# A decoder block in fp32 parts on one Trainium2 core: later first weight load, another count of unread transposes, one unit in another order, one product on another engine

## The chip, the cores and the metric

The kernel is one program on one core of a Trainium2 chip. The metric is the device time of one execution in microseconds (us). A core has five engines that run their own instruction streams beside each other and wait for each other by semaphores: TensorE (PE in the rows, its weight loads PEld), VectorE (DVE), ScalarE (ACT), GpSimd (POOL) and SyncE (SP), which here only issues DMA transfers.

## The reference

One layer of a hybrid block on x of 512 tokens by 1024 channels, all in float32. Cut to what matters:

```python
h = rms_norm(x, pre_mix_g)
q, k, v, u_pool, u_conv, g_logits = split(h @ w_in)
attn = moba_attention(q, k, v, rel_bias) @ w_attn_o
pool = pool_mixer(u_pool, w_pool_g, pool_scale) @ w_pool_o
conv = conv_module(u_conv, w_dw, b_dw, ln_g, ln_b) @ w_conv_o
gates = sigmoid(g_logits + b_gate)
x = x + rms_norm((gates[0]*attn + gates[1]*pool + gates[2]*conv) @ w_out, post_mix_g)
h = rms_norm(x, pre_ffn_g)
gt, up = split(h @ w_ffn_in)
f = (silu(gt) * up) @ w_ffn_out
out = x + rms_norm(f, post_ffn_g)
```

The two places of the change are the very first line with the first products behind it (the two halves of u_conv), and the last line.

## The kernel before

Every product is made of three matmuls on parts: a value is split into a high part (rounded by ScalarE on the way through a copy) and a low part (what is left, a subtraction on VectorE), and hi by hi, hi by lo and lo by hi are added up in one PSUM bank. A unit is one weight tile of 1024 by 128: it is loaded into one of the three slots of `raw` by SP (line 323), ScalarE writes `w_hi` (598) and VectorE `w_lo` (1004), and TensorE runs 8 steps k of three matmuls of 512 columns (1556 to 1558).

**The start.** SP issues the four token tiles of 128 tokens (`x_tok`, 326), then the weight loads of units 0 to 2 with the vector table `vec` behind the first of them (336), then four small loads. For each token tile ScalarE squares and sums (617), GpSimd takes the power -0.5 (451), VectorE scales the tile (1027) and TensorE turns it in eight transposes (1572), one into each PSUM bank. Between them stand unread transposes of the identity into bank 5 (1577): 20 in front of tile 0, 5 in front of tiles 2 and 3, none in front of tile 1. Behind the last tile's eighth transpose the same transpose is repeated 14 times. Then, bank by bank, ScalarE writes `h_hi` (629) and VectorE `h_lo` (1037), and unit 0 begins as soon as the first of these is there. Of the low parts of units 0 and 1 VectorE writes the first half and GpSimd the second (455). TensorE starts a unit when `lo_done` says that the low part is there; within units 0 and 1 it waits for GpSimd's half at step 4.

**The end.** The last product (f by w_ffn_out) is built as seven half-size products in 39 units; the sums of the products are four quadrants of the output, c11, c12, c21 and c22 (tokens by channels, halves each), where c22 is finished during unit 35. ScalarE squares a quadrant's two tiles and sums them, the gain vector `post_ffn_g` is multiplied in, and at the very end VectorE multiplies by 1/rms and adds the residual (`add_x1`, 1509). GpSimd multiplies c11, c21 and c22 by the gain (572); c12, the last one, is multiplied on VectorE (1544). After the products GpSimd also takes the reciprocal roots (`final_rstd`, 575 to 579). VectorE's queue over the last units is a list written by hand: for each unit n the low part of its weights (`down_lo`, 1451), the low part of the token side (`s_lo`, 1461), and at fixed n the additions to the quadrants. TensorE takes units 36 to 38 first for token tile 0 and then again for token tile 1 (1896 to 1903).

The order on each engine is the order in which the code is written; no scheduler stands between.

Of the kernel before, what the change touches and what calls it, by code (L numbers as in the profile page):

```python
# [29 lines left out]
P = 128  # L30
SEQ = 512
# [104 lines left out]
def build(nc, x, w_in, w_branch, w_out, w_ffn_in, w_ffn_out, vecs, post_mix_g, pre_ffn_g, post_ffn_g,  # L136
# [98 lines left out]
    with ExitStack() as ctx:  # L235
        bank = [ctx.enter_context(nc.psum_tensor(f"bank{i}", [P, SEQ], F32)) for i in range(8)]

        def sem(name):
# [49 lines left out]
            sem("u4_full"), sem("y1_full"), sem("c_gained"), sem("y_gained"), sem("out_ready"))  # L288

# [28 lines left out]
        def _(sp):  # L318
# [8 lines left out]
            first = [COL_CONV + 256, COL_CONV, COL_CONV + 384, COL_CONV + 128, COL_POOL, COL_POOL + 128]  # L327
            for u, col in enumerate(first):
# [6 lines left out]
                if u == 0:  # L335
                    sp.dma_start(vec[:, :], vecs).then_inc(vec_full, 16)
# [99 lines left out]
        def _(pool):  # L436
# [132 lines left out]
            for i, (c, half) in enumerate(((c11, 0), (c21, 0), (c22, 1))):  # L569
                for t in range(2):  # L570
                    pool.wait_ge(sq_done, 16 + 2 * i + t + 1)
                    pool.tensor_tensor(c[:, t, :], c[:, t, :], gain[:, half * SEQ:(half + 1) * SEQ], ALU.mult)\  # L572
                        .then_inc(c_gained, 1)
# [426 lines left out]
        def _(dve):  # L1000
# [511 lines left out]
            for n in range(2, DOWN_UNITS):  # L1512
# [19 lines left out]
                if n == C22_MADE:  # L1532
                    dve.wait_ge(p_moved, 6)
                    add_product(c22, PH_P7)

            for t in range(2):
                dve.wait_ge(rstd_done, 12 + t + 1)
                dve.wait_ge(c_gained, 6)
                add_x1(c21, t, 2 + t, 0)
                add_x1(c22, t, 2 + t, 1)  # L1540
# [12 lines left out]
        def _(pe):  # L1553
# [20 lines left out]
            for t in range(TOK):  # L1574
                if t != 1:
                    for _ in range(5 if t else 20):
                        pe.transpose(bank[5][:, SEQ - P:SEQ], ident[:, :], ident[:, :])
                pe.wait_ge(xn_done, t + 1)
                for k in range(KT):
                    ins = turn_tile(t, k)  # L1580
                    if t == TOK - 1:
                        if k == KT - 1:
                            for _ in range(14):
                                ins = turn_tile(t, k)
                        ins.then_inc(xt_done, 1)
# [3 lines left out]
            def first_k(u):  # L1589

                def before(k):
                    if u == 0:
                        pe.wait_ge(h_lo_done, k + 1)
                    if k == KT // 2:
                        pe.wait_ge(low_rest_done, u + 1)
                return before

            for u in range(FIRST_UNITS):
                pe.wait_ge(lo_done, u + 1)
                if u >= RING:  # L1600
                    pe.wait_ge(*FIRST_FREED[u - RING])
                unit(u % RING, bank[u % RING], h_hi, h_lo, before_k=first_k(u) if u < 2 else None).then_inc(unit_done, 1)
# [368 lines left out]
```

## Time and profile before

| | us |
|---|---|
| median of 3 runs (708.35 to 708.84) | 708.79 |
| the profiled execution | 707.53 |
| its span, first to last instruction | 705.3 |
| TensorE busy | 695.8 |
| VectorE busy | 533.8 |
| ScalarE busy | 359.6 |
| GpSimd busy | 238.0 |

The profiled execution is 1.26 us shorter than the median; every number from the trace belongs to it. Starts are in us from the first instruction. A matmul row has a start and a modelled duration that overlaps the next one, so the distance from start to start is the pace, and a hole is a distance above it. A duration on VectorE or GpSimd includes what the instruction waits for after its start.

### The profile page before, as it was taken

How to read it: one execution, taken by the hardware profiler on the slowest of the kernel's cores; microseconds unless marked ns; L12 is line 12 of the kernel's file. 1: busy time of each engine (PE TensorE's matmuls, PEld its weight loads, DVE VectorE, ACT ScalarE, POOL GpSimd, SP SyncE). 2: the span in 40 equal slices, each digit the busy share in tenths (PEclk: the TensorE clock that was granted, in tenths of full speed). 3: DMA queues.
4: the chain of work that ended last, by engine and by line, in shares of the span. 5: the costliest groups of instructions: out<-in, count | busy, mean ns of one | idle time of the engine just before them, and what ended most of it. 6: DMA issues, size and time to landing. Idle time of an engine off the chain costs nothing.

```text
span 705.3 us, 11497 instructions
## 1 busy us (share of the span) xinstructions
PE 695.8 (99%) x4056; PEld 616.8 (87%) x4056; DVE 533.8 (76%) x776; ACT 359.6 (51%) x582; POOL 238.0 (34%) x213
## 2 busy tenths in 40 slices
PE   8999999999999999999999999999999999999996
PEld 7888888888888888888889999999999999888884
DVE  5338878578666666788478988887888787898997
ACT  7235544544544655234367454555455546655672
POOL 3842211112220000562222556665566550000125
PEclk9999999999999999999999999999999999999999
DMA  6158899999985213234403133313322334665563
GB/s 247 60 210 237 226 238 227 233 267 217 231 206 148 93 61 119 90 100 162 192 26 120 60 120 119 105 74 119 119 103 76 119 119 151 191 196 199 169 206 127
DMA packets 37678, 107.24 MB, mean 152 GB/s; under 512 B 4041, under 2 KB 4041, under 8 KB 37457
## 3 DMA queue, kind: packets, MB, share of 16 engines
q1 hardware_dynamic: 29648, 83.79, 34.4%
q0 software_dynamic: 8000, 23.07, 15.2%
q8 instruction: 17, 0.28, 0.2%
q14 instruction: 13, 0.10, 0.0%
HBM read 104.73 MB, written 25.19 MB: 184 GB/s over the span
## 4 chain that ended last, share of the span: by engine, by line
PE 96%; DVE 1%; DMA 1%; ACT 0%; issue 0%; POOL 0%; SPq 0%; DVEq 0%; POOLq 0%; ACTq 0%
PE bank L1556 30%; PE bank L1558 30%; PE bank L1557 30%; PE bank L1622 1%; DMA x_tok<-in_x_dram 1%; PE bank L1612 1%; PE bank L1613 1%; PE bank L1639 1%; PE bank L1638 1%; DVE w_lo L1451 1%; PE bank L1766 1%; PE bank L1572 0%; DVE s_lo L1461 0%; PE bank L1629 0%; DVE c L1500 0%
## 5 line engine op out<-in xcount | busy, mean ns | idle before, releaser
L1556 PE MATMUL bank<-h_hi,w_hi 128*128 128x512 f32 (+1 forms) x392 | 149.6, 382 | 0.0
L1558 PE MATMUL bank<-h_hi,w_lo 128*128 128x512 f32 (+1 forms) x392 | 147.6, 377 | 0.0
L1557 PE MATMUL bank<-h_lo,w_hi 128*128 128x512 f32 (+1 forms) x392 | 147.5, 376 | 0.0
L1004 DVE TENSOR_TENSOR w_lo<-raw,w_hi 128x1024 fp32r<-128x1024 f32 (+1 forms) x54 | 70.6, 1308 | 58.5 <-ACT w_hi L606 46.2
L1558 PEld LDWEIGHTS bank<-h_hi,w_lo 128*128 128x128 f32 x392 | 73.8, 188 | 13.7
L1556 PEld LDWEIGHTS bank<-h_hi,w_hi 128*128 128x128 f32 x392 | 73.8, 188 | 13.0 <-DVE w_lo L1004 0.4
L1557 PEld LDWEIGHTS bank<-h_lo,w_hi 128*128 128x128 f32 x392 | 73.9, 188 | 12.6
L1556 PE MATMUL bank<-tm_hi,blk_hi 128*128 128x256 f32 x240 | 67.9, 283 | 0.0
L1557 PE MATMUL bank<-tm_lo,blk_hi 128*128 128x256 f32 x240 | 67.9, 283 | 0.0
L1558 PE MATMUL bank<-tm_hi,blk_lo 128*128 128x256 f32 x240 | 67.9, 283 | 0.0
L1385 DVE TENSOR_TENSOR blk_lo<-raw_pair,blk_hi 128x512 fp32r<-128x512 f32 (+1 forms) x40 | 59.5, 1488 | 7.4 <-ACT blk_hi L863 7.4
L1556 PE MATMUL bank<-w_hi,s_hi 128*128 128x512 f32 x154 | 60.1, 390 | 0.9 <-DVE s_lo L1461 0.9
L863 ACT ACTIVATE blk_hi<-raw_pair 128x512 fp32r<-128x512 f32 (+1 forms) x40 | 33.7, 841 | 52.5 <-DVE raw_pair L1391 52.5
L555 POOL TENSOR_TENSOR w_sum<-raw_pair 128x512 f32<-128x512 f32 x20 | 32.2, 1612 | 83.4 <-DMA raw_pair<-in_w_ffn_in_dram 83.4
L1557 PE MATMUL bank<-w_lo,s_hi 128*128 128x512 f32 x154 | 59.9, 389 | 0.0
L1558 PE MATMUL bank<-w_hi,s_lo 128*128 128x512 f32 x154 | 59.9, 389 | 0.0
L888 ACT ACTIVATE w_hi<-raw 128x1024 fp32r<-128x1024 f32 (+1 forms) x39 | 40.9, 1049 | 33.1 <-PE bank L1558 33.1
L1451 DVE TENSOR_TENSOR w_lo<-raw,w_hi 128x1024 fp32r<-128x1024 f32 (+1 forms) x39 | 50.1, 1284 | 9.9 <-ACT w_hi L888 9.8
L606 ACT ACTIVATE w_hi<-raw 128x1024 fp32r<-128x1024 f32 x46 | 48.4, 1052 | 3.9 <-PE bank L1558 3.7
L572 POOL TENSOR_TENSOR c<-c,gain 128x512 f32<-128x512 f32 x6 | 11.5, 1931 | 103.3 <-ACT junk L617 103.3
L1556 PEld LDWEIGHTS bank<-tm_hi,blk_hi 128*128 128x128 f32 x240 | 46.1, 192 | 0.0
L1557 PEld LDWEIGHTS bank<-tm_lo,blk_hi 128*128 128x128 f32 x240 | 46.1, 192 | 0.0
(233 smaller groups left out, 1779.8 us busy)
## 6 DMA issues: line engine op xcount, KB each, us to landing
raw<-in_w_in_dram SPq DMA_DIRECT2D x42, 512.0 KB, 4.9
raw_pair<-in_w_ffn_in_dram SPq DMA_DIRECT2D x40, 512.0 KB, 3.7
comb<-in_w_ffn_out_dram POOLq DMA_DIRECT2D x30, 512.0 KB, 7.1
raw<-comb SPq DMA_DIRECT2D x20, 512.0 KB, 3.6
raw<-in_w_ffn_out_dram SPq DMA_DIRECT2D x15, 512.0 KB, 3.7
comb<-comb POOLq DMA_DIRECT2D x10, 512.0 KB, 5.1
raw<-in_w_branch_dram SPq DMA_DIRECT2D x8, 512.0 KB, 3.2
raw<-in_w_out_dram SPq DMA_DIRECT2D x8, 512.0 KB, 3.2
```

What stands on the lines that cost most here:

```text
L555: pool.tensor_tensor(w_sum[:, 0, :], m21, m22, ALU.add).then_inc(w_summed, 1)
L572: pool.tensor_tensor(c[:, t, :], c[:, t, :], gain[:, half * SEQ:(half + 1) * SEQ], ALU.mult)\
L606: act.activation(w_hi[:, hslot, :], raw[:, slot, :], ACT.Copy).then_inc(hi_done, 1)
L863: act.activation(dst, src, ACT.Copy).then_inc(blk_hi_done, 1)
L888: act.activation(w_hi[:, down_slot(n), used], raw[:, u % RING, used], ACT.Copy).then_inc(hi_done, 1)
L1004: dve.tensor_tensor(dst, src_hi[0], src_hi[1], ALU.subtract).then_inc(lo_done, 1)
L1385: dve.tensor_tensor(dst, src, part.bitcast(F32), ALU.subtract).then_inc(blk_lo_done, 1)
L1451: dve.tensor_tensor(w_lo[:, down_slot(n), used], raw[:, u % RING, used], w_hi[:, down_slot(n), used].bitcast(F32), ALU.subtract).then_inc( ...
L1556: pe.matmul(dst, a_hi, b_hi, start=start, stop=False, skip_group_check=resumed)
L1557: pe.matmul(dst, a_hi, b_lo, start=False, stop=False, skip_group_check=resumed)
L1558: return pe.matmul(dst, a_lo, b_hi, start=False, stop=stop, skip_group_check=resumed)
L1612: pe.matmul(bank[3 + i % 2][:, 0:w], q_parts[:, head, q], k_hi2[:, head, 0:w], start=True, stop=False)
```

## The change

Four edits. (1) SP: `vec` is loaded directly behind the token tiles, and the three weight loads wait until token tile 1 has landed (`x_full[1]`). (2) TensorE: the unread transposes are 27, 0, 3, 3 in place of 20, 0, 5, 5, and the last tile's repeats are 7 in place of 14. (3) TensorE: unit 1 runs its 16 matmuls with the high part of the weights first, waiting for that part alone, and then the 8 with the low part. (4) The product of c22 by the gain moves from GpSimd to VectorE, one token tile behind unit 36 and the other behind unit 37, under a new semaphore.

```diff
+            sp.dma_start(vec[:, :], vecs).then_inc(vec_full, 16)
+            sp.wait_ge(x_full[1], 16)
             for u, col in enumerate(first):
...
-                if u == 0:
-                    sp.dma_start(vec[:, :], vecs).then_inc(vec_full, 16)
...
-            for i, (c, half) in enumerate(((c11, 0), (c21, 0), (c22, 1))):
+            for i, c in enumerate((c11, c21)):
                 for t in range(2):
                     pool.wait_ge(sq_done, 16 + 2 * i + t + 1)
-                    pool.tensor_tensor(c[:, t, :], c[:, t, :], gain[:, half * SEQ:(half + 1) * SEQ], ALU.mult)\
+                    pool.tensor_tensor(c[:, t, :], c[:, t, :], gain[:, 0:SEQ], ALU.mult)\
                         .then_inc(c_gained, 1)
...
+                if n in (C22_MADE + 1, C22_MADE + 2):
+                    t = n - C22_MADE - 1
+                    dve.wait_ge(sq_done, 16 + 4 + t + 1)
+                    dve.wait_ge(gain_full, 48)
+                    dve.tensor_tensor(c22[:, t, :], c22[:, t, :], gain[:, SEQ:], ALU.mult).then_inc(c22_gained, 1)
...
-                dve.wait_ge(c_gained, 6)
+                dve.wait_ge(c_gained, 4)
                 add_x1(c21, t, 2 + t, 0)
+                dve.wait_ge(c22_gained, t + 1)
                 add_x1(c22, t, 2 + t, 1)
...
-                    for _ in range(5 if t else 20):
+                    for _ in range(3 if t else 27):
...
-                            for _ in range(14):
+                            for _ in range(7):
...
+            def high_parts_first(u):
+
+                pe.wait_ge(hi_done, u + 1)
+                for k in range(KT):
+                    w1 = w_hi[:, u % RING, k * P:(k + 1) * P]
+                    pe.matmul(bank[u % RING][:, :], w1, h_hi[:, k, :], start=k == 0, stop=False)
+                    pe.matmul(bank[u % RING][:, :], w1, h_lo[:, k, :], start=False, stop=False)
+                pe.wait_ge(lo_done, u + 1)
+                for k in range(KT):
                     if k == KT // 2:
                         pe.wait_ge(low_rest_done, u + 1)
-                return before
+                    ins = pe.matmul(bank[u % RING][:, :], w_lo[:, u % RING, k * P:(k + 1) * P], h_hi[:, k, :],
+                                    start=False, stop=k == KT - 1)
+                return ins
...
+                if u == 1:
+                    high_parts_first(u).then_inc(unit_done, 1)
+                    continue
```

SP's queue at the start, before; `x_tok` are the token tiles, `raw` the weight slots:

```order
L326 DMA x_tok<-in_x_dram 128x1024 x4
L323 DMA raw<-in_w_in_dram 128x1024
L336 DMA vec<-in_vecs_dram 128x102
L323 DMA raw<-in_w_in_dram 128x1024 x2
L338 DMA table<-in_rel_bias_dram 8x32
```

and after the change:

```order
L327 DMA x_tok<-in_x_dram 128x1024 x4
L329 DMA vec<-in_vecs_dram 128x102
L324 DMA raw<-in_w_in_dram 128x1024 [waits x_full1]
L324 DMA raw<-in_w_in_dram 128x1024 x2
L339 DMA table<-in_rel_bias_dram 8x32
```

The load of vec stands ahead of the first weight load, which waits for token tile 1; all that SP issues behind it moves with it.

TensorE from the last matmul of unit 0 on, before; w_hi and w_lo are the parts of the weights, h_hi and h_lo those of the tokens:

```order
L1558 MATMUL bank<-h_hi,w_lo 128x512
L1556 MATMUL bank<-h_hi,w_hi 128x512 [waits lo_done]
L1557 MATMUL bank<-h_lo,w_hi 128x512
L1558 MATMUL bank<-h_hi,w_lo 128x512
L1556 MATMUL bank<-h_hi,w_hi 128x512
L1557 MATMUL bank<-h_lo,w_hi 128x512
```

and after the change:

```order
L1565 MATMUL bank<-h_hi,w_lo 128x512
L1606 MATMUL bank<-h_hi,w_hi 128x512 [waits hi_done]
L1607 MATMUL bank<-h_lo,w_hi 128x512
L1606 MATMUL bank<-h_hi,w_hi 128x512
...
L1607 MATMUL bank<-h_lo,w_hi 128x512
L1612 MATMUL bank<-h_hi,w_lo 128x512 [waits lo_done]
L1612 MATMUL bank<-h_hi,w_lo 128x512 x3
L1612 MATMUL bank<-h_hi,w_lo 128x512 [waits low_rest_done]
L1612 MATMUL bank<-h_hi,w_lo 128x512 x3
L1563 MATMUL bank<-h_hi,w_hi 128x512 [waits lo_done]
```

The wait for the low part has moved from the first matmul of unit 1 to its seventeenth.

VectorE behind the additions that finish c22 (`c_110` in these rows), before:

```order
L1451 TENSOR_TENSOR w_lo<-raw,w_hi 128x1024 [waits hi_done]
L1461 SCALAR_TENSOR_TENSOR s_lo<-s_116,s_hi 128x512 [waits s_hi_done]
L1451 TENSOR_TENSOR w_lo<-raw,w_hi 128x1024 [waits hi_done]
L1461 SCALAR_TENSOR_TENSOR s_lo<-s_116,s_hi 128x512 [waits s_hi_done]
L1451 TENSOR_TENSOR w_lo<-raw,w_hi 128x512 [waits hi_done]
L1461 SCALAR_TENSOR_TENSOR s_lo<-s_116,s_hi 128x256 [waits s_hi_done]
L1509 SCALAR_TENSOR_TENSOR x_87<-c_112,stat,x_87 128x512 [waits c_gained,rstd_done]
L1509 SCALAR_TENSOR_TENSOR x_87<-c_110,stat,x_87 128x512
L1509 SCALAR_TENSOR_TENSOR x_87<-c_112,stat,x_87 128x512 [waits c_gained,rstd_done]
```

and after the change:

```order
L1452 TENSOR_TENSOR w_lo<-raw,w_hi 128x1024 [waits hi_done]
L1462 SCALAR_TENSOR_TENSOR s_lo<-s_116,s_hi 128x512 [waits s_hi_done]
L1540 TENSOR_TENSOR c_110<-c_110,gain 128x512 [waits gain_full,sq_done]
L1452 TENSOR_TENSOR w_lo<-raw,w_hi 128x1024 [waits hi_done]
L1462 SCALAR_TENSOR_TENSOR s_lo<-s_116,s_hi 128x512 [waits s_hi_done]
L1540 TENSOR_TENSOR c_110<-c_110,gain 128x512 [waits gain_full,sq_done]
L1452 TENSOR_TENSOR w_lo<-raw,w_hi 128x512 [waits hi_done]
L1462 SCALAR_TENSOR_TENSOR s_lo<-s_116,s_hi 128x256 [waits s_hi_done]
L1510 SCALAR_TENSOR_TENSOR x_87<-c_112,stat,x_87 128x512 [waits c_gained,rstd_done]
L1510 SCALAR_TENSOR_TENSOR x_87<-c_110,stat,x_87 128x512 [waits c22_gained]
L1510 SCALAR_TENSOR_TENSOR x_87<-c_112,stat,x_87 128x512 [waits c_gained,rstd_done]
L1510 SCALAR_TENSOR_TENSOR x_87<-c_110,stat,x_87 128x512 [waits c22_gained]
```

Two products stand between the low parts of units 36, 37 and 38, and the first residual additions wait for them.

## Rows read from the trace of the kernel before

**Rows 1.** The page: busy time, share of the span, instructions of each engine.
```profile
PE 695.8 (99%) x4056; PEld 616.8 (87%) x4056; DVE 533.8 (76%) x776; ACT 359.6 (51%) x582; POOL 238.0 (34%) x213
```

**Rows 2.** Timeline, first 9 us: start, duration, engine, line, operation [idle before, releaser].
```profile
0.74 1.82 SPq L326 DMA_DIRECT2D x_tok<-in_x_dram  x4
...
1.53 4.42 PE L1577 MATMUL bank<-ident 128*128 128x128 f32 x20 [1.53 <-POOL ident L439]
...
2.59 0.52 SPq L323 DMA_DIRECT2D raw<-in_w_in_dram  x1
...
5.29 1.06 ACT L617 ACTIVATE junk_x<-x_tok 128x1025 bf16<-128x1025 f32 x1 [0.20 <-DMA x_tok<-in_x_dram]
...
7.09 1.06 ACT L617 ACTIVATE junk_x<-x_tok 128x1025 bf16<-128x1025 f32 x1 [0.65 <-DMA x_tok<-in_x_dram]
...
8.38 1.06 ACT L617 ACTIVATE junk_x<-x_tok 128x1025 bf16<-128x1025 f32 x1
```

**Rows 3.** Tile raw, first 60 us: time from issue to landing of its loads.
```profile
DMA to landing us min/median/max: 3.1/4.6/8.4
```

**Rows 4.** Chain of waits, first 14 us: start, duration, what.
```profile
1.65 5.41 DMA x_tok<-in_x_dram
```

**Rows 5.** Timeline, 9.7 to 13.6 us, all engines.
```profile
9.70 1.06 ACT L598 ACTIVATE w_hi<-raw 128x1024 fp32r<-128x1024 f32 x1 [0.17 <-DMA raw<-in_w_in_dram]
...
10.19 0.75 DVE L1027 TENSOR_SCALAR x_tok<-x_tok,stat 128x1024 f32<-128x1024 f32 x1 [0.54 <-POOL stat L451]
...
10.84 1.84 POOL L455 TENSOR_TENSOR w_lo<-raw,w_hi 128x512 fp32r<-128x512 f32 x1 [0.68 <-ACT w_hi L598]
10.86 0.68 DVE L1004 TENSOR_TENSOR w_lo<-raw,w_hi 128x512 fp32r<-128x512 f32 x1
...
11.18 2.56 PE L1572 MATMUL bank<-ident,x_tok 128*128 128x128 f32 x22
11.55 4.74 ACT L629 ACTIVATE h_hi<-bank,vec 128x512 fp32r<-128x512 f32 x8 [0.80 <-PE bank L1572]
12.36 5.36 DVE L1037 SCALAR_TENSOR_TENSOR h_lo<-bank,vec,h_hi 128x512 fp32r<-128x512 f32 x8 [0.81 <-ACT h_hi L629]
...
13.51 0.48 PE L1556 MATMUL bank<-h_hi,w_hi 128*128 128x512 f32 x1
```

**Rows 6.** Tile h_lo, first 20 us: the eight operations, ns minimum, median, maximum.
```profile
L1037 DVE SCALAR_TENSOR_TENSOR h_lo<-bank,vec,h_hi x8: 736/740/750, 12.4 to 17.0; 128x512 fp32r<-128x512 f32 x8
```

**Rows 7.** Timeline, 17.3 to 19.6 us, where unit 0 ends and unit 1 starts.
```profile
17.32 1.31 POOL L455 TENSOR_TENSOR w_lo<-raw,w_hi 128x512 fp32r<-128x512 f32 x1 [4.63 <-ACT w_hi L598]
...
17.64 1.53 DVE L1004 TENSOR_TENSOR w_lo<-raw,w_hi 128x512 fp32r<-128x512 f32 x1
...
18.84 0.39 PE L1558 MATMUL bank<-h_hi,w_lo 128*128 128x512 f32 x1
...
19.22 0.50 PE L1556 MATMUL bank<-h_hi,w_hi 128*128 128x512 f32 x1
...
19.56 0.39 PE L1557 MATMUL bank<-h_lo,w_hi 128*128 128x512 f32 x1
```

**Rows 8.** Timeline, 687 to 693 us, VectorE and POOL.
```profile
687.70 1.22 DVE L1451 TENSOR_TENSOR w_lo<-raw,w_hi 128x1024 fp32r<-128x1024 f32 x1
...
688.22 3.54 POOL L572 TENSOR_TENSOR c<-c,gain 128x512 f32<-128x512 f32 x2 [8.77 <-ACT junk L617]
...
688.83 1.79 DVE L1461 SCALAR_TENSOR_TENSOR s_lo<-s,s_hi 128x512 fp32r<-128x512 f32 x1
...
690.54 2.31 DVE L1451 TENSOR_TENSOR w_lo<-raw,w_hi 128x1024 fp32r<-128x1024 f32 x1
...
692.77 0.68 DVE L1461 SCALAR_TENSOR_TENSOR s_lo<-s,s_hi 128x512 fp32r<-128x512 f32 x1
```

**Rows 9.** Timeline, 692 to 694 us, TensorE: the stall.
```profile
692.27 0.39 PE L1558 MATMUL bank<-w_hi,s_lo 128*128 128x512 f32 x1
...
693.59 0.47 PE L1556 MATMUL bank<-w_hi,s_hi 128*128 128x512 f32 x1 [0.94 <-DVE s_lo L1461]
```

More of the change, by code:

```diff
@@ L288, in build @@
             sem("u4_full"), sem("y1_full"), sem("c_gained"), sem("y_gained"), sem("out_ready"))
+        c22_gained = sem("c22_gained")
         comb_step = [sem("comb_step0"), sem("comb_step1")]
@@ L1587, in _, with first_k @@
                     ins.then_inc(xt_done, 1)
[L1589 to L1593, printed above, removed]
+            def first_k(k):
+                pe.wait_ge(h_lo_done, k + 1)
+                if k == KT // 2:
+                    pe.wait_ge(low_rest_done, 1)
+            def high_parts_first(u):
[6 more added lines that the diff above has]
+                for k in range(KT):
                     if k == KT // 2:
                         pe.wait_ge(low_rest_done, u + 1)
-                return before
+                    ins = pe.matmul(bank[u % RING][:, :], w_lo[:, u % RING, k * P:(k + 1) * P], h_hi[:, k, :],
+                                    start=False, stop=k == KT - 1)
+                return ins
             for u in range(FIRST_UNITS):
+                if u == 1:
+                    high_parts_first(u).then_inc(unit_done, 1)
+                    continue
                 pe.wait_ge(lo_done, u + 1)
@@ L1601, in _ @@
                     pe.wait_ge(*FIRST_FREED[u - RING])
-                unit(u % RING, bank[u % RING], h_hi, h_lo, before_k=first_k(u) if u < 2 else None).then_inc(unit_done, 1)
+                unit(u % RING, bank[u % RING], h_hi, h_lo, before_k=None if u else first_k).then_inc(unit_done, 1)
             def scores(p, i):
```

## The prediction, made before the changed kernel ran

> **What bounds the kernel now.** I read the page's busy times first: TensorE is busy for 99% of the span [rows 1], and in the trace its matmuls follow each other without a hole, apart from the ends of the program. The only ways to a shorter run are therefore fewer matmuls, which the change does not bring to the real work, or less time at the two ends and at joints between units. So I next read the timeline of the first 20 us, in order of dependence. The four token tiles are issued from 0.74 on, the first weight unit at 2.59 [rows 2]; ScalarE squares tile 1 from 5.29 (it had waited for the transfer), tile 2 from 7.09 (again behind the transfer) and tile 3 from 8.38, directly behind tile 2 [rows 2]. ScalarE takes the high parts of unit 0 from 9.70, released by their transfer [rows 5], which so took 7.1 us from its issue. Then three things happen in a chain: tile 3 is normalised (10.19 to 10.94), its transposes start at 11.18, ScalarE forms the first h_hi at 11.55, VectorE the first h_lo at 12.36, and the first real matmul starts at 13.51 [rows 5]. Last I read the last 20 us: one stall of TensorE, between matmul starts at 692.27 and 693.59, put down to the s_lo of VectorE [rows 9].
>
> **Unread transposes.** They are matmuls into bank 5 or repeats of one tile, whose results nothing uses. (a) Behind the last token tile 14 repeats become 7. The first h_lo, one of eight of 0.74 us [rows 6], is complete at 12.36 + 0.74 = 13.10, and with 0.06 us for the hand-over the first matmul could start at 13.16; it starts at 13.51, since TensorE is still in its 22 transposes [rows 5]. Half of the repeats take away 7 x 0.11 = 0.8 us (22 transposes in 2.56 us, 0.11 each), so the cover is gone and all of 0.35 us is gained; more is not, since h_lo is then last. (b) Before tiles 2 and 3 five become three. Tile 3 is ready at 10.94, its transposes start at 11.18; without an obstacle the hand-over takes about 0.06. That gives 0.18 us. (c) In front of tile 0, 20 become 27. Twenty take 4.42 us from 1.53 [rows 2], 0.22 each, twice the 0.11 of the later ones. Seven more reach to 7.5 at the first pace and to 6.7 at the second. Tile 0 itself is not on the path (the chain of waits begins with the transfer of tile 2 [rows 4]), and tiles 0 and 1 have until 9.7, so I cost this at nothing; at the slow pace all through it would push the later transposes by up to 0.6 us.
>
> **The first weight load behind the second token tile.** Three weight loads (units 0 to 2, then the small table, constants and pooling weights behind them on SP's queue) move from 2.59 to about 5.3, when tile 1 has landed; the vector load (vec) goes ahead of them. What can be gained is that tiles 2 and 3 land sooner. The bound is the ScalarE queue: tile 1's square starts at 5.29, tile 2's could follow 1.3 us later at 6.6 instead of 7.09, tile 3's at 7.95 instead of 8.38. So between 0 and 0.43 us; I take 0.2, since the loads moved are behind tiles 2 and 3 in one queue anyway. What it can cost is the weights' own arrival, L. From L on the path is: high part 1.06, low first half on VectorE, and then the first h_lo can start; in the trace that VectorE subtraction starts at 10.86 and takes 0.68 [rows 5]. High parts start at L, so h_lo starts at about L + 1.9 and the matmul 0.8 later, at L + 2.7. With L = 9.7 + 0.1 for the vec load that now stands ahead, this is 12.5. The path through tile 3 is 13.51 - 0.35 - 0.18 - 0.2 = 12.78. The later one counts: the weights keep 0.3 us in hand, and the first matmul starts at **12.78**, a gain of **0.73 us** (0.53 at no help to the tiles, 0.96 at full help). The loads pushed later have room: unit 1 is wanted at 16, the pooling weights at 17, the table after 18.7, where POOL ends its share of unit 1 at 17.32 + 1.31 [rows 7].
>
> The Trainium skill, "DMA: Bandwidth & Descriptors", section "Queues, rings and completion order", says that on each DMA engine the descriptors of one issuing engine's ring are consumed in ring order. By it the weight load could not have delayed token tiles issued before it, the help is nil, and the head gains 0.53. No row of before separates the two; it is rival B.
>
> **Unit 1, high parts first.** Unit 0's last matmul starts at 18.84, unit 1's first two at 19.22 and 19.56: 0.72 us for two intervals, which within unit 0 are 0.23 each (23 of them from 13.51 to 18.84) [rows 5, 7]. The wait is for the low half that VectorE takes from 17.64 to 19.17 (1.53 us instead of 0.68, beside POOL's 17.32 to 18.63). After the change the first 16 matmuls (3.6 us) need only the high part, which was ready before POOL started at 17.32. The low part then has 3 us in hand. The number of matmuls is the same, 24. Gain **0.27 us**. What is late next is ScalarE's high part, due at about 17.3 - 0.6 against a unit 0 that ends at 18.3: 1.5 us in hand.
>
> **c22 by the gain on VectorE.** Now POOL multiplies both halves of c22 from 688.22 to 691.76; beside it VectorE's s_lo takes 1.79 us and its w_lo 2.31, where the same forms take 0.68 and 1.22 without POOL [rows 8]. The two stretches cost 1.1 + 1.1 = 2.2 us of VectorE's time, and unit 37's s_lo ends at 693.45, too late. After the change VectorE takes two more operations of 128 x 512 (nearest row: the subtraction of that form, 0.68 [rows 5, 8]; issue to issue 0.6). Its queue becomes: s_lo of unit 36 at 688.83, product 689.43, w_lo 690.03, s_lo of unit 37 at 691.2, done 691.9; second product 691.8, w_lo 692.4, s_lo of unit 38 at 693.0, done 693.4. TensorE wants unit 37 at 692.50 (its pitch after 692.27) and unit 38 six matmuls later at 693.86. Both are met by 0.5 us. So the whole stall goes: 693.59 - 692.50 = 1.09, and 0.11 for the slow interval behind a restart, as from 19.22 to 19.56 (0.34 against 0.23) [rows 7, 9]: **1.2 us**. Behind the last matmul the chain is square, mean, power, add and store, in which nothing moves. The new waits on VectorE: the first product waits for ScalarE's square, which released POOL at 688.22, before VectorE gets there; the gain vector came long before. POOL, freed of 3.5 us, forms the reciprocal roots earlier, at worst when VectorE leaves it a gap.
>
> **Sum.** 0.73 + 0.27 + 1.2 = **2.2 us**. The profiled execution took 707.53 us (span 705.3), so it would take 705.3. The median of the runs shown is 708.79, 1.26 above it; on that level the forecast is **706.6 us**. Between the ends nothing moves: TensorE is at its pitch, and the queues that feed it follow it.
>
> **Rivals.** *B, ring order:* tiles 2 and 3 do not land sooner. 0.53 + 0.27 + 1.2 = 2.0, 706.8 us. For it: one queue. Against: tile 2's transfer took 5.41 us where the shortest weight load took 3.1 [rows 3, 4], though the queue holds only two tiles in front of it. *C, POOL takes the port at unit 0's low half.* In the trace both start on it at once (POOL 10.84, VectorE 10.86), and VectorE goes through in 0.68 while POOL needs 1.84; VectorE was still in tile 3's normalisation up to 10.94. At 17.32 POOL was first, and VectorE ended 0.54 after POOL's 1.31 [rows 5, 7]. After the change VectorE may stand idle when the high part ends, and then POOL, 0.02 ahead, may win: low half done at L + 1.06 + 0.1 + 1.31 + 0.54 = 12.8, h_lo from 12.7, matmul at 13.5. The head gains nothing, total 0.27 + 1.2 = 1.5, 707.3 us. The Trainium skill, "SBUF — State Buffer", on the port pair that VectorE and GpSimd share, says that whichever issues first holds it for the whole instruction; by that rule, and POOL's 0.02 us lead, C is the outcome. The rows at 17.32 agree with it, those at 10.84 do not decide. *D, the tail stall stays:* the two products on VectorE, or POOL's small operations that now fall beside them, make unit 37 or 38 late by as much as before. Total 1.0, 707.8 us. For it: only 0.5 us in hand. *E, slower: the weights of unit 0 are the new bound.* Issued at 5.35 with the other two loads directly behind, they take the longest time that a weight load took here, 8.4 us [rows 3], L = 13.75 and the first matmul at 16.45, 2.9 us later than now; less 0.27 and 1.2 that is 1.5 us more than before, 710.3. It decides from L = 12.3 on. Against: the first load took 7.1 us with four token tiles in front of it; in the new place at most two and a half are left.
>
> **How the numbers follow.** Forecast 0.45, B 0.2, C 0.2, D 0.09, E 0.06. The range takes in B, C and D and the upper ends (0.96 + 0.27 + 1.25 = 2.5, 706.3, and 0.9 for the level of the runs): 705.4 to 708.1. About 0.2% (1.4 us) is what a measurement of this kernel can tell from no change, so faster means below 707.4: the forecast and B nearly whole, under half of C, a little of D, 0.70. The same: half of C and most of D, with some of the forecast lost to the level, 0.24. Slower: 0.06.
>
> **What would show it.** First real matmul: 12.8 (forecast), 13.0 (B), 13.5 with a first low half of over 1.5 us on VectorE (C), later with ScalarE waiting for the raw transfer by over a microsecond (E). Tile 2's square before 7.0 speaks against B. No hole of over 0.05 us between units 0 and 1. In the tail no s_lo wait, s_lo and w_lo at 0.7 and 1.2, unit 37's s_lo done 0.5 us before its matmul. The prediction is wrong if TensorE shows a longer pitch anywhere between (fewer unread transposes, and a slower clock granted behind them), or a new hole at the joint of units 1 and 2.

## The result, and the profile after

| | before | after |
|---|---|---|
| median of 22 runs, us | 708.36 | 706.22 |
| range of these runs | 707.26 to 708.85 | 705.80 to 708.65 |
| the profiled execution | 707.53 | 706.34 |
| its span | 705.3 | 704.3 |

The ratio of after to before is 0.9973, with a 95% interval of 0.9967 to 0.9979: 2.14 us of the medians, where 2.2 was forecast. In absolute terms 706.6 us was forecast and 706.22 came. The two profiled executions differ by 1.19 us only. Both differences are right, and why they are not the same is the main thing that the experiments brought out.

The page of the changed kernel; columns as in [rows 1]:

```profile
PE 694.5 (99%) x4052; PEld 615.9 (87%) x4052; DVE 533.7 (76%) x778; ACT 359.5 (51%) x582; POOL 232.7 (33%) x211
```

VectorE is as busy as before (533.8 us then), although it has two more operations, and GpSimd has 5.3 us less.

The waits of TensorE in the changed kernel (line waited for: us in total, times, longest). The wait for s_lo in the tail, of 0.9 us before, is gone; what is left lies in the head:

```profile
PE bank L1579 <- DVE x_tok L1028: 1.9, 2, 1.3
PE bank L1584 <- POOL ident L440: 1.5, 1, 1.5
PE bank L1563 <- DVE h_lo L1038: 0.3, 1, 0.3
```

The head of the changed kernel, to be held against [rows 2] and [rows 5]:

```profile
0.74 1.82 SPq L327 DMA_DIRECT2D x_tok<-in_x_dram  x4
...
1.53 4.55 PE L1584 MATMUL bank<-ident 128*128 128x128 f32 x27 [1.53 <-POOL ident L440]
...
5.32 1.45 SPq L324 DMA_DIRECT2D raw<-in_w_in_dram  x3
...
8.03 1.06 ACT L618 ACTIVATE junk_x<-x_tok 128x1025 bf16<-128x1025 f32 x1 [1.56 <-DMA x_tok<-in_x_dram]
...
9.34 1.06 ACT L618 ACTIVATE junk_x<-x_tok 128x1025 bf16<-128x1025 f32 x1 [0.15 <-DMA x_tok<-in_x_dram]
...
10.84 1.06 ACT L599 ACTIVATE w_hi<-raw 128x1024 fp32r<-128x1024 f32 x1 [0.35 <-DMA raw<-in_w_in_dram]
...
11.93 0.69 DVE L1005 TENSOR_TENSOR w_lo<-raw,w_hi 128x512 fp32r<-128x512 f32 x1
...
11.96 1.86 PE L1579 MATMUL bank<-ident,x_tok 128*128 128x128 f32 x15
11.97 1.78 POOL L456 TENSOR_TENSOR w_lo<-raw,w_hi 128x512 fp32r<-128x512 f32 x1 [0.86 <-ACT w_hi L599]
12.38 3.58 ACT L630 ACTIVATE h_hi<-bank,vec 128x512 fp32r<-128x512 f32 x6 [0.49 <-PE bank L1579]
13.19 2.73 DVE L1038 SCALAR_TENSOR_TENSOR h_lo<-bank,vec,h_hi 128x512 fp32r<-128x512 f32 x4 [0.57 <-ACT h_hi L630]
...
14.08 0.47 PE L1563 MATMUL bank<-h_hi,w_hi 128*128 128x512 f32 x1 [0.27 <-DVE h_lo L1038]
```

Tile 2 is squared from 8.03 and tile 3 from 9.34, a microsecond later than in the trace of before (7.09, 8.38). The high part of unit 0 starts at 10.84, the first real matmul at 14.08, which is 0.57 us later than the 13.51 of before. The 27 unread transposes in front are over in 4.55 us, at 6.1; the forecast had put their end between 6.7 and 7.5.

The joint of units 0 and 1 (compare [rows 7]):

```profile
18.14 1.30 POOL L456 TENSOR_TENSOR w_lo<-raw,w_hi 128x512 fp32r<-128x512 f32 x1 [4.39 <-ACT w_hi L599]
...
18.46 1.53 DVE L1005 TENSOR_TENSOR w_lo<-raw,w_hi 128x512 fp32r<-128x512 f32 x1
...
19.43 0.39 PE L1565 MATMUL bank<-h_hi,w_lo 128*128 128x512 f32 x1
...
19.65 0.39 PE L1606 MATMUL bank<-h_hi,w_hi 128*128 128x512 f32 x1
...
19.88 0.39 PE L1607 MATMUL bank<-h_lo,w_hi 128*128 128x512 f32 x1
```

The wait for the low part is there as before (POOL 1.30, VectorE 1.53), and TensorE does not see it: 19.43, 19.65, 19.88.

VectorE and GpSimd in the tail (compare [rows 8]), and TensorE at unit 37 and at the very last matmul (compare [rows 9]):

```profile
687.96 1.21 DVE L1452 TENSOR_TENSOR w_lo<-raw,w_hi 128x1024 fp32r<-128x1024 f32 x1
...
689.09 0.68 DVE L1462 SCALAR_TENSOR_TENSOR s_lo<-s,s_hi 128x512 fp32r<-128x512 f32 x1
...
689.31 0.52 POOL L583 TENSOR_SCALAR stat<-stat 128x4 f32<-128x4 f32 x1 [10.71 <-ACT junk L618]
...
689.69 0.68 DVE L1540 TENSOR_TENSOR c<-c,gain 128x512 f32<-128x512 f32 x1
...
689.95 1.62 POOL L577 TENSOR_SCALAR stat<-stat 128x1 f32<-128x1 f32 x1
...
690.29 1.22 DVE L1452 TENSOR_TENSOR w_lo<-raw,w_hi 128x1024 fp32r<-128x1024 f32 x1
...
691.43 0.68 DVE L1462 SCALAR_TENSOR_TENSOR s_lo<-s,s_hi 128x512 fp32r<-128x512 f32 x1
...
692.03 0.68 DVE L1540 TENSOR_TENSOR c<-c,gain 128x512 f32<-128x512 f32 x1
```

```profile
692.53 0.39 PE L1565 MATMUL bank<-w_hi,s_lo 128*128 128x512 f32 x1
692.76 0.39 PE L1563 MATMUL bank<-w_hi,s_hi 128*128 128x512 f32 x1
...
697.97 0.39 PE L1565 MATMUL bank<-w_hi,s_lo 128*128 128x512 f32 x1
```

Here s_lo takes 0.68 where it took 1.79, and w_lo 1.22 where it took 2.31. The two products by the gain are the rows at 689.69 and 692.03. Unit 37's s_lo is done at 692.11 and its first matmul starts at 692.76, in step with the one before it. What waits now is GpSimd: its operation on one column at 689.95 takes 1.62 us beside VectorE's low parts, where the same form takes 0.27 at 699.19.

### The profile page after: what moved, and what is told of

It reads as the page before. It is cut to its first block, busy times and chain, and to the rows that moved or that the text cites. A ratio compares the mean times of both kernels' runs of the same rounds, so it can differ in the third digit from the quotient of the medians.

```text
span 704.3 us, 11491 instructions
## 1 busy us (share of the span) xinstructions
PE 694.5 (99%) x4052; PEld 615.9 (87%) x4052; DVE 533.7 (76%) x778; ACT 359.5 (51%) x582; POOL 232.7 (33%) x211
## 4 chain that ended last, share of the span: by engine, by line
PE 97%; DMA 1%; ACT 0%; DVE 0%; POOL 0%; SPq 0%; issue 0%; DVEq 0%; POOLq 0%; ACTq 0%
PE bank L1563 30%; PE bank L1565 30%; PE bank L1564 30%; PE bank L1643 1%; DMA x_tok<-in_x_dram 1%; PE bank L1633 1%; PE bank L1634 1%; PE bank L1660 1%; PE bank L1659 1%; PE bank L1787 1%; PE bank L1607 0%; PE bank L1612 0%; PE bank L1606 0%; PE bank L1650 0%; PE bank L1579 0%; ACT junk_x L618 0%
## 5 line engine op out<-in xcount | busy, mean ns | idle before, releaser
L1563 PE MATMUL bank<-h_hi,w_hi 128*128 128x512 f32 (+1 forms) x384 | 146.3, 381 | 0.3 <-DVE h_lo L1038 0.3
L1565 PE MATMUL bank<-h_hi,w_lo 128*128 128x512 f32 (+1 forms) x384 | 144.5, 376 | 0.0
L1564 PE MATMUL bank<-h_lo,w_hi 128*128 128x512 f32 (+1 forms) x384 | 144.4, 376 | 0.0
L1565 PEld LDWEIGHTS bank<-h_hi,w_lo 128*128 128x128 f32 x384 | 72.3, 188 | 13.4
L1563 PEld LDWEIGHTS bank<-h_hi,w_hi 128*128 128x128 f32 x384 | 72.3, 188 | 12.8 <-issue 0.5
L1564 PEld LDWEIGHTS bank<-h_lo,w_hi 128*128 128x128 f32 x384 | 72.4, 188 | 12.3
L1565 PEld LDWEIGHTS bank<-tm_hi,blk_lo 128*128 128x128 f32 x240 | 46.1, 192 | 0.0
```

The lines of the kernel that those rows point to most:

```text
L1563: pe.matmul(dst, a_hi, b_hi, start=start, stop=False, skip_group_check=resumed)
L1564: pe.matmul(dst, a_hi, b_lo, start=False, stop=False, skip_group_check=resumed)
L1565: return pe.matmul(dst, a_lo, b_hi, start=False, stop=stop, skip_group_check=resumed)
```

## The experiments

### Two more traces of the same two kernels

No edit.

> The kernel before, unchanged, for a second trace of its head. If the landing of token tiles 2 and 3 belongs to the program, they are squared at 7.1 and 8.4 again and the first real matmul starts at 13.5. If it varies from run to run, this trace lies elsewhere by several tenths of a microsecond; the median of the timed runs of before (708.36) against its profiled 707.53 lets expect a later start, 14.0 to 14.4.

> The changed kernel, unchanged, for a second trace of its head. If the landing belongs to the program, tile 2 is squared at 8.0 again and the first real matmul starts at 14.1. If it varies, elsewhere by several tenths. Its timed median (706.22) is near its profiled 706.34, so 14.0 is what its own times let expect.

Measured: `before_again` took 708.62 us, with tile 2 squared from 8.23 and the first real matmul at 14.65, later still than the 14.0 to 14.4 expected; the first trace of the same program had 7.09 and 13.51. `after_again` took 706.23 us, with 7.92 and 13.97. When the second half of the tokens lands varies from run to run by more than a microsecond, and the trace of before that the prediction was read from was a lucky one.

This gives a way to compare kernels without that luck. In every trace in which the tokens and not the weights set the start of unit 0, the time of the execution is the start of tile 2's square plus a constant of the kernel. The constant says nothing of when tile 2 lands, only what follows behind it:

| kernel | tile 2 squared from | first real matmul | last matmul | execution | execution less tile 2 |
|---|---|---|---|---|---|
| before | 7.09 | 13.51 | 698.93 | 707.53 | 700.44 |
| before_again | 8.23 | 14.65 | 700.02 | 708.62 | 700.39 |
| late_load_only | 7.10 | 13.56 | 698.89 | 707.52 | 700.42 |
| unread_only | 7.87 | 13.92 | 699.71 | 708.31 | 700.44 |
| high_first_only | 7.82 | 14.24 | 699.36 | 707.96 | 700.14 |
| unread_and_high_first | 8.09 | 14.14 | 699.36 | 707.96 | 699.87 |
| tail_only | 6.95 | 13.37 | 697.65 | 706.02 | 699.07 |
| after_early_load | 7.48 | 13.51 | 697.42 | 705.79 | 698.31 |
| after | 8.03 | 14.08 | 697.97 | 706.34 | 698.31 |
| after_again | 7.92 | 13.97 | 697.86 | 706.23 | 698.31 |
| after_no_unread_front | 7.92 | 13.99 | 697.86 | 706.23 | 698.31 |

In the two kernels traced twice the constant repeats to 0.05 us. Between kernels it is to be read to a tenth: in late_load_only tile 3 is squared 1.46 us behind tile 2, where it is 1.29 in before, and the constant came out the same even so. From before to after it falls by 700.42 - 698.31 = 2.11 us, and that is the effect of the change behind the landing. Whether the landing itself moved, only the timed runs can say. By these constants the two medians belong to nearly the same one: 708.36 - 700.42 = 7.94 and 706.22 - 698.31 = 7.91.

### The fourth edit alone

```diff
-            for i, (c, half) in enumerate(((c11, 0), (c21, 0), (c22, 1))):
+            for i, c in enumerate((c11, c21)):
...
+                if n in (C22_MADE + 1, C22_MADE + 2):
...
+                    dve.tensor_tensor(c22[:, t, :], c22[:, t, :], gain[:, SEQ:], ALU.mult).then_inc(c22_gained, 1)
```

> The kernel before with the fourth edit alone: c22 by the gain on VectorE in place of GpSimd, two products behind units 36 and 37. Theory (the prediction's step): the stall of TensorE before unit 37 goes whole, the ratio to before is 0.9983 (1.2 us less), unit 37's s_lo is done 0.5 us before its first matmul, and s_lo and w_lo of units 36 and 37 take 0.7 and 1.2 us. Rival (the products only move the lateness): the stall is still there, under 0.3 us gained, ratio above 0.9995.

Measured: 707.05 us median over 9 runs against 708.36, ratio 0.9981 [0.9971, 0.9991]. The stall before unit 37 is gone. From unit 36's last matmul in front of the stall to the very last one it is 697.65 - 692.22 = 5.43 us, against 698.93 - 692.27 = 6.66: 1.23 us less. In all six traces without this edit that stretch is 6.63 to 6.67 us, in all seven with it 5.44 to the hundredth, as read from the unrounded starts. From the first to the last matmul it is 684.28 us against 685.42, 1.14 less, since this trace lost 0.08 us in front of the stall, which the changed kernel did not. The constant falls by 1.35. The other 0.2 us lies outside the span: execution less span is 2.2 to 2.3 us in all runs without this edit (707.53 - 705.3, 708.62 - 706.4, 707.96 - 705.7 in the traces) and 1.95 to 2.1 in all runs with it (706.02 - 704.0, 706.34 - 704.3, 705.79 - 703.8). The theory holds, the rival falls.

### The unread transposes alone

```diff
-                    for _ in range(5 if t else 20):
+                    for _ in range(3 if t else 27):
...
-                            for _ in range(14):
+                            for _ in range(7):
```

> The kernel before with the second edit alone: unread transposes 27, 0, 3, 3 and 7 repeats in place of 20, 0, 5, 5 and 14. Theory (the prediction's steps a and b): 0.53 us less, ratio 0.9993, and the first real matmul starts 0.1 us behind the first h_lo instead of 0.4. Rival (fewer unread transposes cost the clock): matmuls of unit 0 start 0.46 us apart instead of 0.23 for some microseconds, the kernel is slower by 1 us or more.

Measured: 708.21 us against 708.29, ratio 0.9996 [0.9987, 1.0005]; constant 700.44, as before. From tile 2's square to the first real matmul it is 13.92 - 7.87 = 6.05 us, against 13.51 - 7.09 = 6.42: the edit does bring 0.37 us there, where the theory had 0.53. The waits of TensorE in this kernel show where it goes:

```profile
PE bank L1556 <- DVE h_lo L1037: 0.3, 1, 0.3
PE bank L1556 <- DVE w_lo L1004: 0.2, 1, 0.2
```

The first is the new wait for the first h_lo, as forecast. The second is the joint of units 0 and 1: it now opens by 0.61 us from start to start (19.27 to 19.88), where it was 0.38. The chain of waits runs there through VectorE, which is not earlier by what TensorE has gained:

```profile
17.73 0.66 DVE h_lo L1037
18.38 1.45 DVE w_lo L1004
```

So 0.23 of the 0.37 us is given back at the joint. What is left, 0.14, is about what VectorE itself gained on tile 2's square (0.12). It too is missing from the constant, and most of it, 0.10, goes in one place: TensorE turns the tile `prob` between two matmuls that start at 204.49 and 205.51, 1.02 us apart, against 203.81 and 204.72, 0.91 apart, in before. unread_and_high_first, with the same edit, has 0.91 there, so this loss is not shown to belong to the edit; the timed runs (0.08 us between the medians) do not settle so small a thing. The matmuls of unit 0 are 0.23 us apart; the rival with the clock falls.

### High parts first alone

```diff
+            def high_parts_first(u):
...
+                if u == 1:
+                    high_parts_first(u).then_inc(unit_done, 1)
+                    continue
```

> The kernel before with the third edit alone: unit 1 with its high parts first. Theory (the prediction's step): the hole between units 0 and 1 goes, 0.27 us less, ratio 0.9996, unit 1's first two matmuls 0.23 us apart. Rival (the wait comes back at the low parts or at unit 2): no difference, and a hole of 0.2 us or more at the seventeenth matmul of unit 1 or at the first of unit 2.

Measured: 708.03 us against 708.29, ratio 0.9995 [0.9986, 1.0004]; constant 700.14, which is 0.28 us less than before's 700.42. No start-to-start distance above 0.25 us is left between 18 and 26 us, so neither is there one at the joint of units 1 and 2. The timed runs alone do not settle so small a thing; the constant and the closed hole do, and the rival (the wait comes back later) falls.

### Both of these

The kernel before with the two edits above.

> The kernel before with edits two and three (unread transposes, high parts first) and neither of the others. Alone, the unread transposes brought the first matmul 0.37 us nearer to tile 2's square, but the hole between units 0 and 1 grew from 0.38 to 0.61; alone, high parts first closed a hole of 0.27. Theory A (the third edit also gets back what the second lost at the joint): execution minus the start of tile 2's square is 700.42 - 0.37 - 0.27 = 699.8 or less, and no hole at the joint. Theory B (the two add up as each alone): 700.1 to 700.2.

Measured: 707.54 us against 708.15, ratio 0.9992 [0.9982, 1.0001]; constant 699.87, so 0.55 us less than before. Each alone brings -0.02 and 0.28. The value lies much nearer to theory A's 699.8 than to theory B's 700.1: the third edit keeps the second's gain, which is lost at the joint without it.

### The late load alone

```diff
+            sp.dma_start(vec[:, :], vecs).then_inc(vec_full, 16)
+            sp.wait_ge(x_full[1], 16)
             for u, col in enumerate(first):
...
-                if u == 0:
-                    sp.dma_start(vec[:, :], vecs).then_inc(vec_full, 16)
```

> The kernel before with the first edit alone: vec directly behind the token tiles, the weight loads once tile 1 has landed. In six traces so far tile 2 was squared from 7.09, 8.23, 6.95 and 7.48 us with the early load, and from 8.03 and 7.92 with the late one. Theory A (the prediction's step, the tiles land sooner): 0.2 us less, ratio 0.9997. Theory B (it helps nothing): ratio 1.0000 within 0.3 us, and tile 2 squared near 8.0. Theory C (it narrows the spread of the landing): the timed runs lie within 0.8 us of each other, where those of before lie within 1.6.

Measured: 708.36 us against 708.29, ratio 0.9997 [0.9988, 1.0006], runs from 707.43 to 708.90; constant 700.42, the same as before. The medians show nothing gained, as in theory B, but the interval is 0.6 us to either side, so theory A's 0.2 is not excluded. The trace itself has an early landing, 7.10, against theory B's 8.0; theory C falls, the spread is as wide as it was. The trace also answers the question of the shared port (the prediction's rival C):

```profile
7.10 1.06 ACT L617 ACTIVATE junk_x<-x_tok 128x1025 bf16<-128x1025 f32 x1 [0.60 <-DMA x_tok<-in_x_dram]
...
10.70 1.06 ACT L598 ACTIVATE w_hi<-raw 128x1024 fp32r<-128x1024 f32 x1 [0.98 <-DMA raw<-in_w_in_dram]
...
11.66 4.14 ACT L629 ACTIVATE h_hi<-bank,vec 128x512 fp32r<-128x512 f32 x7
11.79 0.69 DVE L1004 TENSOR_TENSOR w_lo<-raw,w_hi 128x512 fp32r<-128x512 f32 x1 [0.66 <-ACT w_hi L598]
11.83 1.79 POOL L455 TENSOR_TENSOR w_lo<-raw,w_hi 128x512 fp32r<-128x512 f32 x1 [1.49 <-ACT w_hi L598]
```

Here VectorE had been idle when the high part ended. It starts its half 0.04 us ahead of GpSimd and goes through in 0.69 us, and GpSimd takes 1.79.

### The changed kernel with the early load

```diff
-            sp.dma_start(vec[:, :], vecs).then_inc(vec_full, 16)
-            sp.wait_ge(x_full[1], 16)
...
+                if u == 0:
+                    sp.dma_start(vec[:, :], vecs).then_inc(vec_full, 16)
```

> The changed kernel with the loads in their old place: weight loads of units 0 to 2 at once behind the token tiles, the vector table behind the first of them. In the profile of the changed kernel token tile 2 was squared from 8.03 us and tile 3 from 9.34, against 7.09 and 8.38 before, and the weights of unit 0 landed only at 10.8. Theory A (the late load costs at the head): this kernel is faster than the changed one, tile 2 squared at 7.1, first real matmul near 13.0, total 0.7 to 1.1 us less than the changed kernel's profile. Theory B (the prediction's step: the late load helps the tiles by 0.2 us): it is 0.2 us slower than the changed kernel. Theory C (when the tiles land varies from run to run, whatever the load does): the two do not differ by more than 0.3 us in the medians.

Measured: 706.37 us over 7 runs, ratio to before 0.9972 [0.9961, 0.9983], where the changed kernel has 0.9973; constant 698.31, to the hundredth that of the changed kernel. The medians differ by 0.15 us, as theory C has it, and 7.48 in this trace is one more draw of the landing. Theory A, 0.7 to 1.1 us faster, falls. A 0.2 us either way (theory B) lies within what these runs leave open: the constant can't show it, since it starts at the landing.

### Weights behind tile 3, and tile 3 behind tile 0

If neither place of the weight load matters to be seen, what does tile 2 wait for? Two more kernels go at the suspects: no weight byte at all beside the tiles, and tile 3 issued some 2 us later.

```diff
-            sp.wait_ge(x_full[1], 16)
+            sp.wait_ge(x_full[3], 16)
```

> The changed kernel with the weight loads issued only when tile 3 has landed, so that no weight byte can be in the way of a token tile. Theory A (weight bytes delay tiles 2 and 3 even in the changed kernel): tile 2 is squared before 7.0 us and tile 3 before 8.3. Theory B (the tiles delay each other, or the small rows of vec do): tile 2 is still squared at 7.9 to 8.0, tile 3 at 9.2. In both the weights of unit 0 land at tile 3's landing plus 3.2 us, 11 to 12.5, and by the prediction's L + 2.7 the first real matmul starts at 14 to 15.2: 0 to 1.2 us more than the changed kernel.

Measured: 706.71 us, ratio 0.9979 [0.9970, 0.9988], and in the trace:

```profile
7.28 1.06 ACT L618 ACTIVATE junk_x<-x_tok 128x1025 bf16<-128x1025 f32 x1 [0.70 <-DMA x_tok<-in_x_dram]
...
11.87 1.06 ACT L599 ACTIVATE w_hi<-raw 128x1024 fp32r<-128x1024 f32 x1 [2.15 <-DMA raw<-in_w_in_dram]
...
13.62 2.07 DVE L1038 SCALAR_TENSOR_TENSOR h_lo<-bank,vec,h_hi 128x512 fp32r<-128x512 f32 x3
...
14.52 0.47 PE L1563 MATMUL bank<-h_hi,w_hi 128*128 128x512 f32 x1 [1.48 <-DVE h_lo L1038]
```

With no weight byte in flight tile 2 is squared from 7.28, inside the 6.95 to 8.23 of the other kernels, neither theory's number. What the run does settle is the path through the weights. They land at 11.87, h_lo starts 1.75 us and the first matmul 2.65 us later; the prediction had L + 1.9 and L + 2.7. The first matmul is 0.44 and 0.55 us later than in the two traces of the changed kernel, inside the 0 to 1.2 expected.

```diff
             for t in range(TOK):
+                if t == TOK - 1:
+                    sp.wait_ge(x_full[0], 16)
                 sp.dma_start(x_tok[:, t, 0:D_MODEL], ...
```

> The changed kernel with token tile 3 issued only when tile 0 has landed (about 4.1 us in place of 2.1), the rest as it is. In all traces so far the execution is as long as the start of tile 2's square plus a constant of the kernel (698.3 for the changed kernel), and that start lies between 6.95 and 8.23 us with early and with late weights. Theory A (tile 3's bytes, in flight beside tile 2's, are what holds tile 2 up): tile 2 is squared at 6.5 to 6.9, tile 3 directly behind it, and the median is 0.5 to 1 us below the changed kernel's 706.22, provided tile 3 lands by 7.9. Theory B (tile 2 waits for something else, a slow DMA engine or the load on the memory): tile 2 is squared at 7.5 to 8.2 as before and the median is 706.2 or, if tile 3 now lands later than tile 2's square ends, above it.

Measured: 705.99 us over 6 runs, ratio 0.9969 [0.9957, 0.9981]. In the trace:

```profile
5.32 1.06 ACT L620 ACTIVATE junk_x<-x_tok 128x1025 bf16<-128x1025 f32 x1
...
7.73 1.06 ACT L620 ACTIVATE junk_x<-x_tok 128x1025 bf16<-128x1025 f32 x1 [1.26 <-DMA x_tok<-in_x_dram]
...
11.28 1.06 ACT L601 ACTIVATE w_hi<-raw 128x1024 fp32r<-128x1024 f32 x1 [1.06 <-DMA raw<-in_w_in_dram]
...
13.93 0.47 PE L1565 MATMUL bank<-h_hi,w_hi 128*128 128x512 f32 x1 [0.38 <-DVE h_lo L1040]
```

Tile 2 waits until 7.73 although tile 3 was issued only when tile 0 had landed, at about 4.1: theory B, as far as one trace of a landing that varies can tell. The weights, now landing at 11.28, set the first matmul (again L + 2.65). The median is 0.2 us under the changed kernel's, and before itself is 0.2 lower beside these runs (708.15 against 708.36); the intervals of the two ratios overlap, so this is not shown to be a better kernel.

What goes along with the landing is the rate of the transfers themselves between 5 and 6 us. The same stretch in the two traces of before (busy times by engine, granted clock, DMA share, GB/s), first `before`, with tile 2 from 7.09, then `before_again`, with 8.23:

```profile
5.00:6.00 1.00, 0.95 (x5) 0.66 (x4) 0.16 (x1) 0.80 (x3) 0.56 (x1) 1.00 0.97 377
```

```profile
5.00:6.00 1.00, 0.94 (x5) 0.65 (x4) 0.00 (x0) 0.88 (x3) 0.56 (x1) 1.00 0.79 279
```

and in `late_load_only` (7.10) and `unread_only` (7.87):

```profile
5.00:6.00 1.00, 1.00 (x5) 0.66 (x4) 0.00 (x0) 0.90 (x3) 0.56 (x1) 1.00 1.02 397
```

```profile
5.00:6.00 1.00, 1.00 (x6) 1.00 (x6) 0.04 (x1) 0.73 (x3) 0.56 (x1) 1.00 0.85 287
```

At 377 and 397 GB/s tile 2 is early, at 279 and 287 it is late, by one program or by another. It is not a strict law over all traces (tile3_behind_tile0 has 385 and 7.73, unread_and_high_first 217 and 8.09), and why the rate differs from run to run was not found.

### Without the unread transposes in front

```diff
-                if t != 1:
-                    for _ in range(3 if t else 27):
+                if t == 0:
+                    for _ in range(3):
```

> The changed kernel with 3 unread transposes in front of tile 0 and none in front of tiles 2 and 3; the 7 repeats stay. It measures what the unread transposes buy. Theory A (TensorE is at half its pace for its first microseconds of work, and they move these in front of the tokens): the transposes of tiles 0 to 2 are 0.21 us apart instead of 0.12, some matmuls of unit 0 are 0.43 us apart, and the kernel is 1 to 3 us slower than the changed one. Theory B (the real transposes are work enough): the pace is 0.23 from the first matmul on and the difference is within 0.2 us.

Measured: 706.23 us over 7 runs, ratio 0.9971 [0.9960, 0.9982]; constant 698.31, the changed kernel's own.

```profile
1.53 0.90 PE L1584 MATMUL bank<-ident 128*128 128x128 f32 x3 [1.53 <-POOL ident L440]
...
6.74 3.68 PE L1579 MATMUL bank<-ident,x_tok 128*128 128x128 f32 x16 [4.31 <-DVE x_tok L1028]
...
10.54 1.10 PE L1579 MATMUL bank<-ident,x_tok 128*128 128x128 f32 x8
...
11.87 1.86 PE L1579 MATMUL bank<-ident,x_tok 128*128 128x128 f32 x15 [0.23 <-DVE x_tok L1028]
...
13.99 0.47 PE L1563 MATMUL bank<-h_hi,w_hi 128*128 128x512 f32 x1 [0.27 <-DVE h_lo L1038]
...
14.30 0.39 PE L1564 MATMUL bank<-h_lo,w_hi 128*128 128x512 f32 x1
```

The 16 transposes of tiles 0 and 1 are slow now, 0.22 us apart, as in theory A, but they are not on the path. The 8 of tile 2, behind them, are 0.11 to 0.17 us apart, and tile 3's likewise; the first matmuls are 0.3 and 0.23 apart, as in the changed kernel: theory B in its result. The granted clock of the profile is 1.00 in the slow stretch too (6.5 to 8.5 us), so these rows show the pace and not its reason. Of the unread transposes in front of the token tiles, 27 bought nothing over 3 in these 7 runs; what the 20 of before bought was not tried.

## Why the prediction was right, point by point

**The sum.** 2.2 us forecast, 2.11 measured by the constants and 2.14 by the medians. Its terms came out so:

| term | forecast | measured | from |
|---|---|---|---|
| unread transposes, to the first matmul | 0.53 | 0.37 | 6.42 to 6.05 behind tile 2's square |
| late load, tiles land sooner | 0.2 | not seen | medians 708.36 against 708.29, 706.22 against 706.37; 0.2 is within their noise |
| joint of units 0 and 1 | 0.27 | 0.28 | high_first_only |
| the stall in the tail, inside the span | 1.2 | 1.22 | 6.66 to 5.44 us (692.27 to 698.93, 692.53 to 697.97) |
| outside the span | none | 0.2 | execution less span |

That the total came within 0.1 us is in part luck. The head was forecast at 0.73 and brought 0.37, and 0.2 of what was missing came from outside the span, where nothing had been forecast. The total lies between the forecast's 2.2 and rival B's 2.0, and the timed runs cannot choose between the two.

**Unread transposes: mechanism right, 0.37 where 0.53 was put.** The step that failed is the 0.06 us of hand-over. The first h_lo ends at 13.19 + 0.74 = 13.93 and the matmul starts at 14.08, 0.15 later, so what TensorE's own transposes had cost was 0.25 and not 0.35. The shorter stretch in front of tile 3 brought 0.12 (from 5.27 to 5.15 us between tile 2's square and the first h_lo) where 0.18 was put. And alone this edit was worth next to nothing: the prediction costed the four edits one by one and did not ask whether VectorE, at the joint, would move along. It took the joint's 0.27 as fixed, when the earlier start of unit 0 makes the hole 0.23 wider. With the third edit beside it this did no harm, since that edit closes the wider hole as well: 700.44 to 699.87 is 0.57.

**The late load: the step that no run bore out.** "What can be gained is that tiles 2 and 3 land sooner" rested on one trace, whose tile 2 had in fact landed early. No run shows the gain, and none excludes 0.2. Rival B, no help, fits the runs at least as well. The rule behind it, the Trainium skill, "DMA: Bandwidth & Descriptors", section "Queues, rings and completion order" (descriptors in ring order on each engine), gives a zero; the medians do not contradict it, but tile 2 also comes at 7.73 with tile 3 held back, so there was perhaps no delay for ring order to prevent, and it is not shown to be the reason. The sign "first real matmul at 12.8" was missed by far, 14.08, and is of no use while the landing varies so much.

The feared cost was also misjudged in its base: the weights were put at L = 9.8, they came at 10.84 and 10.78. Their 0.3 us in hand became 0.6, because the tiles were late as well. What this may cost is the fastest runs. With the weights from 10.70 to 10.84, as in the four traces of this load order, the path through them (2.65 us in load_behind_tile3) lets the first matmul start at 13.35 at the earliest, so that the changed kernel would gain nothing from a tile 2 squared before 7.3 (13.35 - 6.05). By its constant, before has 13 of its 89 recorded runs under 7.3; the 29 runs of the changed kernel and of after_no_unread_front have none. This is not shown to be the cost of the late load: no run was made for it, and after_early_load has too few (7, none under 7.3).

**The joint: right**, in place and size. The first distance is 0.22 us (19.43 to 19.65), and at the joint of units 1 and 2, named as a sign of being wrong, no hole opened.

**The tail: right.** Stretches of 1.79 and 2.31 went back to 0.68 and 1.22, unit 37's s_lo was done 0.65 us before its matmul (0.5 forecast). Rival D, the stall stays, fell. GpSimd's small operations do meet VectorE's, and it is they that wait (1.62 us for one column).

**Rival C, GpSimd takes the port first: did not come.** In the changed kernel VectorE started at 11.93 and GpSimd at 11.97; in late_load_only, with VectorE idle before, 11.79 and 11.83. By the rule of the Trainium skill, "SBUF — State Buffer", section "SBUF: two separate sides", that whichever starts first has the shared pair, this is VectorE's win. But the recorded starts do not carry the rule when they are so close: in before (10.84 and 10.86) and in high_first_only (11.57 and 11.59) GpSimd's row starts 0.02 us ahead, and there too VectorE goes through in 0.68 and 0.69 us and GpSimd takes 1.84. The lead of 0.02 us, on which the prediction let C rest, decided nothing.

**Rival E, slower through late weights:** the path is real, and costs L + 2.65 where L + 2.7 was said; load_behind_tile3 runs on it. The landing that would have been needed, 12.3, came in no trace; the latest was 11.87.

**The level.** The forecast was moved up by 1.26 us, from the profiled execution to the median of 3 runs, without a reason. Of this, 0.83 us is the distance to the median of 22 runs, 708.36, and goes with tile 2's landing, 7.09 in that trace and by the constant about 7.9 in the middle of the runs. The other 0.43 us is what those 3 runs were slower than the 22, and it is why 706.6 was forecast and 706.22 came.

## What to carry to other kernels

Before costing an edit of a few tenths, find the one transfer that the path hangs on and see whether its landing repeats; if it does not, compare kernels by their time behind that landing and not by single executions. Such a comparison can't tell whether an edit moves the landing itself; that takes the timed runs. Where a stall of TensorE is put down to a late VectorE operation, look at that operation's length against its normal one: a GpSimd operation beside it can double it, and moving that work to VectorE itself can shorten VectorE's queue. Gains in front of a joint have to be counted through the joint, since the engine that sets it may not move along: here VectorE gained 0.12 us where TensorE gained 0.37.

## What the hardware showed beyond what was expected

- The same four token loads let tile 2 start at 7.09 us in one trace and at 8.23 in another of the same program, with 377 and 279 GB/s moved between 5 and 6 us; over all kernels it is 6.95 to 8.23. Late landings came with the weights and the vector table in either place, and with tile 3 held back; the cause stays open.
- Execution less span was 0.2 us shorter in every kernel with the fourth edit (1.95 to 2.1 against 2.2 to 2.3 in all recorded runs), with nothing in the span to show for it. Why is open.
- TensorE's slow first microseconds (16 transposes in 3.68 us, some 0.2 each, where the next 8 take 1.10) cost nothing here, as they lay in front of the token tile that the path hangs on.
